# Feed-forward gate and up products widened to 512 columns over the high and low half of the input

## The reference

```python
h2 = rms_norm(x, g_ffn[l])                                   # 256 x 1024
gt = causal_dwconv(h2 @ w_ffn_gate[l], ffn_conv_w[l])        # 1024 -> 2816 channels, 3 taps over the tokens
x = x + (jax.nn.silu(gt) * (h2 @ w_ffn_up[l])) @ w_ffn_down[l]
```

## Time and profile before

| | |
|---|---|
| median of 3 runs | 1327.03 us (1326.93 to 1329.15) |
| time of the profiled execution | 1327.21 us |
| its span, from the first to the last instruction | 1325.4 us |
| PE busy / granted TensorE clock | 1301.4 us (98%) / 0.997 |
| DVE busy / ACT busy / POOL busy | 1026.0 us (77%) / 746.5 us (56%) / 47.3 us (4%) |
| mean DMA rate | 169 GB/s |

### The profile page before, as it was taken

One profiled execution on the slowest core, in us unless ns is written; L12 is line 12 of the kernel. 1 busy time (PEld: TensorE's weight loads), 2 busy tenths in 40 slices (PEclk: granted clock), 3 DMA queues, 4 the chain that ended last, 5 costly groups with the idle time before them and its releaser, 6 DMA issues. The chain is left out here.

```text
span 1325.4 us, 26400 instructions
## 1 busy us (share of the span) xinstructions
PE 1301.4 (98%) x10796; PEld 1240.3 (94%) x10796; DVE 1026.0 (77%) x1763; ACT 746.5 (56%) x1149; POOL 47.3 (4%) x48
## 2 busy tenths in 40 slices
PE   9999999999999999999999999999999999999997
PEld 8899999999999999999999989999989899888996
DVE  6899998677777677999997768777778746677565
ACT  6544566556454465544757556544567445586364
POOL 0000000000000000100000000000001100001100
PEclk9999999999999999999999999999999999999999
DMA  8565455565555465646365555665654223343232
GB/s 279 190 201 181 160 161 189 163 220 186 196 191 191 153 229 176 215 162 197 126 210 167 197 184 178 207 203 193 206 163 152 64 97 128 122 143 112 81 101 75
DMA packets 108991, 223.62 MB, mean 169 GB/s; under 512 B 6180, under 2 KB 17700, under 8 KB 108872
## 3 DMA queue, kind: packets, MB, share of 16 engines
q1 hardware_dynamic: 106736, 218.99, 49.5%
q10 hardware_dynamic: 2136, 2.96, 0.7%
HBM read 220.88 MB, written 1.06 MB: 167 GB/s over the span
## 5 line engine op out<-in xcount | busy, mean ns | idle before, releaser
L1191 ACT ACTIVATE whi<-ring 128x1024 fp32r<-128x1024 f32 (+3 forms) x430 | 433.7, 1027 | 343.2 <-PE bank L513 221.3
L1764 DVE TENSOR_TENSOR wlo<-ring,whi 128x1024 fp32r<-128x1024 f32 (+3 forms) x430 | 496.9, 1180 | 166.0 <-ACT whi L1191 133.1
L513 PE MATMUL bank<-hhi,whi 128*128 128x256 f32 x2016 | 272.5, 277 | 2.5 <-ACT hhi L1228 1.8
L522 PE MATMUL bank<-hhi,wlo 128*128 128x256 f32 x2016 | 273.0, 277 | 1.0 <-DVE wlo L1764 1.0
L513 PE MATMUL bank<-hlo,whi 128*128 128x256 f32 x2016 | 269.1, 276 | 0.0
L513 PEld LDWEIGHTS bank<-hhi,whi 128*128 128x128 f32 x2016 | 248.3, 192 | 5.5 <-issue 3.9
L522 PEld LDWEIGHTS bank<-hhi,wlo 128*128 128x128 f32 x2016 | 246.9, 192 | 4.9 <-issue 3.2
L513 PEld LDWEIGHTS bank<-hlo,whi 128*128 128x128 f32 x2016 | 247.3, 193 | 0.0
L1932 DVE SCALAR_TENSOR_TENSOR w<-w,par 128x256 f32<-128x256 f32 x240 | 98.1, 479 | 0.0
L535 PE MATMUL bank<-whi,hhi 128*128 128x512 f32 (+2 forms) x256 | 93.1, 366 | 0.0
L535 PE MATMUL bank<-whi,hlo 128*128 128x512 f32 (+2 forms) x256 | 92.6, 364 | 0.0
(11 more groups left out here) (311 smaller groups left out, 1549.1 us busy)
## 6 DMA issues: line engine op xcount, KB each, us to landing
ring<-in_w_in SPq DMA_DIRECT2D x100, 1024.0 KB, 5.1
ring<-in_w_ffn_down SPq DMA_DIRECT2D x22, 1024.0 KB, 5.1
ring<-in_w_ffn_gate SPq DMA_DIRECT2D x20, 1024.0 KB, 5.1
ring<-in_w_ffn_up SPq DMA_DIRECT2D x20, 1024.0 KB, 5.2
ring<-in_w_merge SPq DMA_DIRECT2D x8, 1024.0 KB, 5.2
ring<-in_w_out SPq DMA_DIRECT2D x8, 1024.0 KB, 5.0
ring<-in_w_oc SPq DMA_DIRECT2D x4, 1024.0 KB, 5.3
ring<-in_w_od SPq DMA_DIRECT2D x4, 1024.0 KB, 5.2
```

Source lines behind the costliest of these rows:

```text
L513: done = e.matmul(o, wh[:, k, cols(u)], paired(s_[:, k0 + k, :]), stop=False, skip_group_check=True, start=opens and k == 0 and s_ is sh a ...
L522: done = e.matmul(o, wl[:, k, cols(u)], paired(sh[:, k0 + k, :]), start=False, stop=closes, skip_group_check=True)
L1191: e.activation(part_of(whi, j), part_raw(j), ACT.Copy).then_inc(*up("hi.a"))
L1764: e.tensor_tensor(part_of(wlo, j), part_raw(j), part_of(whi, j), ALU.subtract).then_inc(*up("lo.v"))
```

## The change

In gate and up, `twice` takes the place of `chans`. `hhi` and `hlo` become two halves of one tensor, `hboth`. A part now holds 4 k for 2 channel blocks. For each k and block one product with 512 moving columns goes over both halves: a bank holds one channel block, `whi`*`hhi` in its left 256 columns and `whi`*`hlo` in its right ones. The third pass adds `wlo`*`hhi` (256 columns) on the left. The first group after the norm (`normed`) keeps products of 256 columns, all of `hhi` first, then all of `hlo`.

A group of two blocks (2 parts) takes two banks, so gate and up of one i6 take the four "m" banks twice over. Each bank's two sides are added on the way out: ACT copies the left side (`highs`), DVE adds the right side to it. Gate goes to `gpad` as before, up to a new buffer `fup`. The first tap moves from DVE to ACT (`first_tap`). The taps of group i now stand behind the emptying of up's group i in DVE's list. The product with up reads `fup` in place of the bank. The last i6 has 4 parts for gate and up, not 8 of half the size. The host stores the two weights in blocks, so that a load of 1 MB is 8 KB in a row for each partition.

```diff
+            def twice(j, held, k0, opens, closes, normed=None):
+                wh, wl = part_of(whi, j), part_of(wlo, j)
+                e.wait_ge(SEM["hi.a"], j + 1)
+                if normed:
+                    for q in range(2):
+                        for k in range(4):
+                            if k % 2 == 0:
+                                e.wait_ge(*at(("hhi", "hlo")[q], *normed, 1, (k0 + k) // 2))
+                            for u in range(2):
+                                done = e.matmul(held[u][:, q * S:q * S + S], wh[:, k, cols(u)], paired(hh[q][:, k0 + k, :]),
+                                                start=opens and k == 0 and q == 0, stop=False, skip_group_check=True)
+                else:
+                    for u in range(2):
+                        for k in range(4):
+                            both = hboth[:, :, k0 + k, :].rearrange("p q (c s) -> p q s c", c=2)
+                            done = e.matmul(held[u][:, 0:2 * S], wh[:, k, cols(u)], both, start=opens and k == 0, stop=False,
+                                            skip_group_check=True)
+                done.then_inc(*up("first.p"))
+                low_ready(j)
+                for u in range(2):
+                    for k in range(4):
+                        done = e.matmul(held[u][:, 0:S], wl[:, k, cols(u)], paired(hhi[:, k0 + k, :]), start=False,
+                                        stop=closes, skip_group_check=True)
                 done.then_inc(*up("second.p"))
...
                     for name in ("gate", "up"):
-                        held = [ps.take(e, "m", name, l, i6, i) for i in range((n + 1) // 2)]
-                        for i in range(4):
-                            chans(j, held, n, hh, 2 * i, i == 0, i == 3,
-                                  normed=("ffn", l) if i6 == 0 and name == "gate" else None)
-                            j += 1
-                        put("second.p", name, l, i6)
+                        for g in range(n // 2):
+                            held = [ps.take(e, "m", name, l, i6, 2 * g + u) for u in range(2)]
+                            for i in range(2):
+                                twice(j, held, 4 * i, i == 0, i == 1,
+                                      ("ffn", l) if i6 == 0 and name == "gate" and g == 0 else None)
+                                j += 1
+                            put("second.p", name, l, i6, g)
...
+                def highs(name, i6, i, dst_of):
+                    e.wait_ge(*at(name, l, i6, i))
+                    if name == "gate":
+                        e.wait_ge(*(at("gtaps", l, i6 - 1, i) if i6 else at("gpad0", l)))
+                    elif i6:
+                        e.wait_ge(*at("fy", l, i6 - 1, i))
+                    for u in range(2):
+                        e.activation(two(dst_of(u)), sides(bank(name, l, i6, 2 * i + u))[0], ACT.Copy).then_inc(*up("ffn.a"))
+                        leave("ffn.a", name, l, i6, 2 * i + u)
+                        put("ffn.a", name, "high", l, i6, 2 * i + u)
...
                     for i in range(n // 2):
-                        bk = bank("gate", l, i6, i)
+                        for _ in range(2):
+                            split_to(j + 4)
+                            j += 1
+                        highs("gate", i6, i, lambda u: gpad[:, i, u, 2:258])
+                        if i:
+                            first_tap(i6, 0)
+                    for i in range(n // 2):
+                        for _ in range(2):
+                            split_to(j + 4)
+                            j += 1
+                        highs("up", i6, i, lambda u: fup[:, 2 * i + u])
                         if i == 0:
...
+                            first_tap(i6, n // 2 - 1)
                     e.wait_ge(*at("gtaps", l, i6, n // 2 - 1))
                     e.activation(fsg[:, 0:n], fy[:, 0:n], ACT.Sigmoid).then_inc(*up("ffn.a"))
...
                     for i in range(n // 2):
-                        last = [None] * 2
-                        e.wait_ge(*at("gpad", l, i6, i))
-                        for k3 in range(3):
+                        for _ in range(2):
+                            split_to(j + 4)
+                            j += 1
+                        for u in range(2):
+                            g2 = two(gpad[:, i, u, 2:258])
+                            e.wait_ge(*at("gate", "high", l, i6, 2 * i + u))
+                            e.tensor_tensor(g2, g2, sides(bank("gate", l, i6, 2 * i + u))[1], ALU.add).then_inc(*up("ffn.v"))
+                            leave("ffn.v", "gate", l, i6, 2 * i + u)
+                        put("ffn.v", "gpad", l, i6, i)
+                    for i in range(n // 2):
+                        for _ in range(2):
+                            split_to(j + 4)
+                            j += 1
+                        for u in range(2):
+                            u2 = two(fup[:, 2 * i + u])
+                            e.wait_ge(*at("up", "high", l, i6, 2 * i + u))
+                            e.tensor_tensor(u2, u2, sides(bank("up", l, i6, 2 * i + u))[1], ALU.add).then_inc(*up("ffn.v"))
+                            leave("ffn.v", "up", l, i6, 2 * i + u)
+                        last = [at("gfirst", l, i6, i)] * 2
+                        for k3 in range(1, 3):
                             for u in range(2):
```

More of the change, by code:

```diff
@@ L61 @@
 MIX_PARTS = 48 + 4 * 12 + 8
-FFN_PARTS = 70
+FFN_PARTS = 66
 TWO_PARTS = 41
@@ L199, in build @@
         posf = sb("posf", [P, 2])
-        hhi = sb("hhi", [P, 8, S], F32R)
-        hlo = sb("hlo", [P, 8, S], F32R)
+        hboth = sb("hboth", [P, 2, 8, S], F32R)
+        hhi, hlo = hboth[:, 0], hboth[:, 1]
         cst = sb("cst", [P, NCN])
@@ L258, in split, with sides @@
             return ap.rearrange("p u (c s) -> p u c s", c=2)
+        def sides(bk):
+            return [ordered(bk[:, q * S:q * S + S])[:, 0] for q in range(2)]
         def blocks(ap):
@@ L428, in build @@
                 for name in ("w_ffn_gate", "w_ffn_up"):
-                    load_k8(by_k(a[name][l]), 512 * i, min(512 * i + 512, FF))
+                    for g in range(2 * i, min(2 * i + 2, 11)):
+                        load(a[name][l, g], [(0, 4, 0, 256), (4, 8, 0, 256)])
                 for i_ in {0: (), 5: (4, 5)}.get(i, (i - 1,)):
@@ L523, in chans @@
                                         skip_group_check=True)
+                done.then_inc(*up("second.p"))
+            def twice(j, held, k0, opens, closes, normed=None):
[21 more added lines that the diff above has]
+                                        stop=closes, skip_group_check=True)
                 done.then_inc(*up("second.p"))
@@ new lines, in first_tap @@
+                def first_tap(i6, i):
+                    e.wait_ge(*at("gpad", l, i6, i))
+                    if i6:
+                        e.wait_ge(*at("f", l, i6 - 1, i))
+                    for u in range(2):
+                        c = 4 * i6 + 2 * i + u
+                        e.activation(fy[:, 2 * i + u], gpad[:, i, u, 0:S], ACT.Copy,
+                                     scale=prm("ffn_w", l, c * 3, c * 3 + 1)).then_inc(*up("ffn.a"))
+                    put("ffn.a", "gfirst", l, i6, i)
@@ L2210, in ffn_v @@
                                 y, g = fy[:, 2 * i + u], gpad[:, i, u, k3:k3 + S]
[L2211 to L2216, removed]
+                                e.wait_ge(*last[u])
+                                e.scalar_tensor_tensor(out=y, in0=g, scalar=wv, in1=y, op0=ALU.mult,
+                                                       op1=ALU.add).then_inc(*up("ffn.v"))
                                 last[u] = now("ffn.v")
                         put("ffn.v", "gtaps", l, i6, i)
-                    for i in range(4):
-                        split_to(j + 4)
-                        j += 1
                     e.wait_ge(*at("fsig", l, i6))
                     e.tensor_tensor(fy[:, 0:n], fy[:, 0:n], fsg[:, 0:n], ALU.mult).then_inc(*up("ffn.v"))
-                    e.wait_ge(*at("up", l, i6))
                     e.wait_ge(*now("ffn.v"))
@@ L2227, in ffn_v @@
                         y2 = fy[:, 2 * i:2 * i + 2]
[L2228 to L2229 removed]
+                        e.tensor_tensor(y2, y2, fup[:, 2 * i:2 * i + 2], ALU.mult).then_inc(*up("ffn.v"))
                         put("ffn.v", "fy", l, i6, i)
@@ L2816 @@
     feed["w_in_2"] = in_pairs(feed["w_in_2"], (0, 416), (3240, 256))
+    for n in ("w_ffn_gate", "w_ffn_up"):
+        feed[n] = np.ascontiguousarray(feed[n].reshape(L, 8, P, 11, 256).transpose(0, 3, 2, 1, 4))
     for n in ("w_merge", "w_ffn_down", "w_out_2"):
```

18 lines of the change are left out of this document (3 added, 15 removed).

## The result

The changed kernel takes 1339.01 us (median of 4, 1336.44 to 1340.49) where the kernel before took 1326.98 in the same runs: ratio 1.0089, 95% interval 1.0076 to 1.0101. Run again later it gave 1.0092 (1.0076 to 1.0108). It is slower by some 12 us. The profiled execution took 1336.44 us, the fastest of the four, 9.2 above the profiled one of before.

What follows compares the result with a forecast made beforehand. TensorE, busy 98% of the span, was taken as the bound. The terms -4.8 + 2.4 + 6.5 + 2.3 + 3.3 = +9.7 us on the profiled 1327.21 us gave 1336.7 us, 0.7% slower, range 1331.0 to 1340.0.

Steps and rivals of the forecast that it cites:

- gain of wide products: Gate and up: a pair of 256-column products made one of 512 saves 7.2 ns; -4.8 us, -5.3 at best.
- bank wait of up 1: Up 1 waits 3.27 us per layer for DVE's adds to free gate 1's banks; +6.5 us.
- waits for the split before gate 2 to 5: TensorE waits 0.30 us for ACT's split at the ends of up 1 to 4, 8 times; +2.4 us.
- start of gate 0: First two parts after the norm wait for its second pair: 0.45, then 0.34 and 0.38 us; +2.3 us.
- low clock: A half-speed stretch behind each bank wait, as TensorE idles over 3 us; +3.3 us (0 to 3.3).
- The chain: Behind the end of up, adds, taps and sigmoid come before the multiply and next splits; 3.46 us later than before.
- T: The time at which TensorE has finished up of one i6.
- The rival with one stretch: Banks wait, but the clock holds (1333.4 us) or falls only once (1335.0); 27%.
- What costs nothing: DVE's extra adds and ACT's copies fit into idle time; a late load lands at T + 18.1, before it is needed.
- the rival with a longer chain or head: Wait before next gate doubles, low stretch follows the norm, or wide products save nothing; 1339 to 1343 us, 9%.
- No bank wait: DVE reaches gate 1's adds by T + 10.48, so up 1 doesn't wait; 1326.9 us, no change, 7%.
- the gain alone: Gain arrives, chain hides, no clock stretch, only gate 0's start costs 1.5; -3.3 us, 1323.7, 5%.

Runs made afterwards that it cites:

- experiment 3: Changed kernel with each wide product taken apart again into two of 256 columns: 1340.90 us, 2.2 above the changed kernel in the same runs.
- gone in 2: Changed kernel with gate of i6 = 1 taking the four spare "s" banks: 1328.91 us, 1.0021 of the kernel before.
- experiment 6: Changed kernel with DVE's taps put ahead of the splits and the emptying of up's group: 1324.82 us, 0.9994 of the kernel before.
- experiment 5: Changed kernel with 14 products of ones into an unused bank just ahead of up 1: 1335.86 us, 2.8 less than the changed kernel.
- experiments 1: The changed kernel run again with no edit: 1338.69 us (1336.42 to 1340.06, 6 runs).
- experiments 4: Changed kernel with 26 products of ones into an unused bank just ahead of up 1: 1337.59 us, up 1 delayed by 2.34 us a layer.
- experiment 9: Kernel before, nothing wide or added, only DVE's taps moved behind the four splits of up: 1355.01 us, 1.022 of the kernel before.
- experiment 7: Changed kernel with both the early taps and the spare "s" banks for gate 1: 1324.56 us, 0.9989 of the kernel before.
- experiment 8: Changed kernel with early taps, spare banks and gate 0's products in the order of the norm: 1323.37 us, 0.9981 of the kernel before.

## Why the prediction was right

The forecast was 1336.7 us in a range of 1331.0 to 1340.0; measured were 1339.0 and 1338.7. The mechanism was right in each part. The sum came out 2.3 us too small, 1.2 in the waits and the rest in the low clock. The sizes, from layers without a low stretch where it is not the clock itself, are these:

| term | forecast | measured | by |
|---|---|---|---|
| gain of wide products | -4.8 | -5.0 | experiment 3 |
| bank wait of up 1 | +6.5 | +6.9 (2 x (3.38 + 0.07)) | profile after; gone in 2 |
| waits for the split before gate 2 to 5 | +2.4 | +3.2 (8 x (0.33 + 0.07)) | profile after; gone in 6 |
| start of gate 0 | +2.3 | +2.5 (2 x 1.24) | profile after |
| sum without the clock | +6.4 | +7.6 (2 x 3.80) | experiment 5: 2 x 183.20 |
| low clock | +3.3 | +1.7 and +4.4 in two profiles; 3 to 6 in the medians | experiments 1, 4, 5 |

- **The gain.** 16 narrow products less 8 wide ones is 0.06 us per part, and the reading over both halves costs nothing. The bound of -5.3 had no working; -5.0 lies inside it. The Trainium skill's isolated spacing ("TensorE: Matmul & The Clock Gate", Part 2, Back-to-back issue gap) would have made it an estimated 1.7 us; the trace agrees with it on 512 columns (216.0 ns) and not on 256 (111.6 for 109).
- **The chain.** Forecast were the multiply at T + 5.00, the split at T + 10.65, the adds at T + 12.93; the trace has 4.99, 10.58, 12.86. That it is the place of the taps is shown from both sides: moved late in the kernel before they bring the same waits (experiment 9), and moved early in the changed one they take back 2.8 of the 3.46 us by which the chain grew (experiment 6).
- **The start of gate 0.** The first part waits 0.50 us for the second pair (315.87 less 314.92, less four products of 0.11) where 0.45 was forecast, the second part 0.70 (2.49 less 1.79) for 0.34 + 0.38.
- **What a wait costs.** This step was too small in each of its ten places: I took 0.06 us for TensorE to see the release, which no row had shown. Up 1 starts 0.26 behind the end of the second add (350.17 + 0.74), gate 2 0.13 behind the end of ACT's split (372.29, the first of the five at 371.23, 1.06 long), and the first products behind a wait are 0.07 slower. That makes 2 x 0.2 + 8 x 0.1 = 1.2 us, which is the whole difference in the sum without the clock. ACT's splits in the profile after:

```profile
371.23 4.84 ACT L1223 ACTIVATE whi<-ring 128x1024 fp32r<-128x1024 f32 x5
```

- **The clock.** One stretch behind each bank wait was the likeliest case, and it was so in one profile of two; in the first, as in narrow's, only layer 1 had it. A clock of 1.00 behind the wait was named as a sign of being wrong, and layer 0 of the first profile has it. The rival with one stretch (1335.0) is what that profile shows (1336.4 with the 1.2 above). So its nearness to the forecast 1336.7 is luck: a stretch too many, 1.6, stands against waits 1.2 too short. The upper bound of 3.3 was too low, since one stretch can cost 2.75. (The stretch of the earlier trace rows was also read too short: the clock in the window from 1170 to 1172 is 0.65, not 1.00, so it begins near 1170.6.) That idleness brings the stretch is shown by experiments 4 and 5. This agrees with the Trainium skill (the same page, Part 1, What's actually happening). It needs no wait of 3 us: experiment 9 has stretches behind 2.19 and 1.84, and the kernel before has one from 1024 behind sixteen products of one column and a wait of 0.24.
- **What costs nothing.** DVE's adds and ACT's copies cost nothing off the chain: in experiment 7 no product of gate, up or down waits after the start of gate 0. One thing was later than I worked out: the load that a late split lets go at T + 13.0 landed not at T + 18.1 but at about T + 20.5 (line 2738's issue at 374.74, ACT's split at 382.18 after 3.54 us of waiting for it). Its product was not due before T + 26, so TensorE never saw it.
- **The rivals.** The median of 1339.0 lies at the lower end of the rival with a longer chain or head, but that isn't what happened: the wait before the next gate is 0.33 and not double 0.30, no low stretch follows the norm, and the wide products save their 5.0. No bank wait and the gain alone did not happen either; but early taps come close to that rival by a changed order.

Open stays why the same wait has a low stretch that begins before TensorE goes on (at 350.1 for 351.23), just after (834.5 for 834.18), or not at all, and why that load took 7.4 us to land where 4.9 is the median of its kind.

## What to carry to other kernels

When products are merged, the banks hold more for less work and must be emptied sooner: look up, for the place with the least cover, what stands in the emptying engine's list ahead of it. An order in an engine's list decides by its chain, not by the engine's share: DVE is 77 or 78% busy in both kernels, yet the order of the taps against the splits and adds behind them is worth 13.9 us, 8.8 of them in plain waits. Before a good idea is given up for a bad time, swap the order first: here the same wide products are 0.9% slower as first written, and in experiment 8 0.2% faster.

## What the runs showed of the hardware

- The same wait of 3.38 us was followed by no, a short or a long stretch at 1.2 GHz: 0, 1.65 or 2.75 us lost. With products of ones in its place none appeared (2 layers each in 2 kernels). Of the ten waits of 1.77 to 2.19 us in experiment 9 two were followed by one.
- A product of ones of 128 columns in 32-bit floats stands in the trace as two records (28 for 14) and takes 0.22 us (5.73 for the 26 of filled_wait), more than a 512-column product of the rounded format at 0.216.
- The first eight products behind a wait take 0.07 us longer than in the stream, and a printed wait in front of them is 0.16 us shorter than the gap between the end by spacing and the next start.
